# Two transformer layers, float32 weights split in two: weight matmuls that name their columns from the last to the first

## What is computed

```python
proj = rms_norm(x) @ w_in                                   # 2048 x 5448
o    = concatenate([mla(...), fox(...)]) @ w_out            # 2048 x 2048
x    = x + rms_norm(o)
x    = x + 0.5 * (silu(h @ w_gate) * (h @ w_up)) @ w_down   # 2048 x 5632, twice; 5632 x 2048
proj = rms_norm(x) @ w_in_2                                 # mixer, 2048 x 11776
x    = x + merged(attention, spatial gate) @ w_out_2
x    = x + 0.5 * (silu(h @ w_gate) * (h @ w_up)) @ w_down   # second feed-forward block
```

## Time and profile before

| | |
|---|---|
| time, median of 3 runs | 2693.84 us (2693.53 to 2694.23) |
| the profiled execution: its time | 2694.18 us |
| its span, first to last instruction | 2692.4 us |
| mean granted TensorE clock | 0.996 |
| PE busy | 2658.2 us, 99% of the span |
| PEld busy | 2209.8 us, 82% |
| DVE busy | 1430.7 us, 53% |
| ACT busy | 1189.7 us, 44% |
| DMA queue of the weights, share of 16 engines | 56.7% |

### The profile page before, as it was taken

The page is one execution under the profiler, slowest core; times in us unless marked ns, Lnnn a source line. Parts: engine busy times, 40 slices in busy tenths (PEclk is TensorE's granted clock), DMA queues, the critical chain, the costliest instruction groups (busy, mean ns, idle before and its releaser), DMA issues.

```text
span 2692.4 us, 32506 instructions
## 1 busy us (share of the span) xinstructions
PE 2658.2 (99%) x12165; PEld 2209.8 (82%) x12165; DVE 1430.7 (53%) x1562; ACT 1189.7 (44%) x1362; POOL 27.0 (1%) x25
## 2 busy tenths in 40 slices
PE   8999999899999999999999999999999999999998
PEld 6888888788888888888888888888888888888886
DVE  6755555654545455455445655555654454544554
ACT  4544554444444443444444554444444444444333
POOL 0000000000000000000000300000000000000000
PEclk9999999999999999999999999999999999999999
DMA  6655545456565655557665445555566665565554
GB/s 196 204 161 171 158 149 194 149 185 191 188 191 188 188 188 193 190 192 232 190 195 187 147 149 180 192 191 190 185 204 190 189 189 187 187 187 194 195 188 149
DMA packets 258672, 496.23 MB, mean 184 GB/s; under 512 B 17602, under 2 KB 19992, under 8 KB 258328
## 3 DMA queue, kind: packets, MB, share of 16 engines
q1 hardware_dynamic: 257040, 489.81, 56.7%
q0 software_dynamic: 896, 4.89, 0.5%
q10 hardware_dynamic: 648, 0.32, 0.0%
HBM read 492.86 MB, written 2.10 MB: 184 GB/s over the span
## 4 chain that ended last, share of the span: by engine, by line
PE 98%; DVE 1%; DMA 0%; ACT 0%; issue 0%; ACTq 0%; DVEq 0%
PE acc L435 94%; PE tr L451 3%; PE s_ps L490 1%; PE o_ps L513 1%; DVE act_lo L1158 0%; DMA fix<-fixed 0%; PE tr L722 0%; DVE xres L1516 0%; ACT act_hi L813 0%; DVE stats L1178 0%; DVE wlo L1126 0%; DVE u L1692 0%; ACT lat L860 0%; DVE xres L1755 0%; DVE xres L1274 0%
## 5 line engine op out<-in xcount | busy, mean ns | idle before, releaser
L1126 DVE TENSOR_TENSOR wlo<-raw,whi 128x1024 fp32r<-128x1024 f32 x929 | 1135.6, 1225 | 1053.6 <-ACT whi L783 1031.1
L783 ACT ACTIVATE whi<-raw 128x1024 fp32r<-128x1024 f32 x929 | 978.9, 1057 | 1107.8 <-PE acc L435 1101.7
L435 PE MATMUL acc<-whi,act_hi 128*128 128x512 f32 (+1 forms) x2560 | 1008.3, 394 | 6.4 <-DVE wlo L1126 4.3
L435 PE MATMUL acc<-whi,act_lo 128*128 128x512 f32 (+1 forms) x2560 | 996.9, 389 | 0.0
L435 PE MATMUL acc<-wlo,act_hi 128*128 128x512 f32 (+1 forms) x2560 | 995.7, 389 | 0.0
L435 PEld LDWEIGHTS acc<-whi,act_hi 128*128 128x128 f32 x2560 | 481.9, 188 | 102.6 <-issue 5.3
L435 PEld LDWEIGHTS acc<-whi,act_lo 128*128 128x128 f32 x2560 | 481.5, 188 | 100.9
L435 PEld LDWEIGHTS acc<-wlo,act_hi 128*128 128x128 f32 x2560 | 482.2, 188 | 95.3
L435 PE MATMUL acc<-whi,h_hi 128*128 128x512 f32 x704 | 274.3, 390 | 0.0
L435 PE MATMUL acc<-whi,h_lo 128*128 128x512 f32 x704 | 274.0, 389 | 0.0
L435 PE MATMUL acc<-wlo,h_hi 128*128 128x512 f32 x704 | 273.9, 389 | 0.0
(11 more groups left out here) (217 smaller groups left out, 1302.3 us busy)
## 6 DMA issues: line engine op xcount, KB each, us to landing
raw<-in_w_in SPq DMA_DIRECT2D x280, 512.0 KB, 3.5
raw<-in_ffn_w_gate SPq DMA_DIRECT2D x176, 512.0 KB, 4.4
raw<-in_ffn_w_up SPq DMA_DIRECT2D x176, 512.0 KB, 4.2
raw<-in_ffn_w_down SPq DMA_DIRECT2D x176, 512.0 KB, 3.7
raw<-in_w_out SPq DMA_DIRECT2D x64, 512.0 KB, 4.1
raw<-in_w_sg_out SPq DMA_DIRECT2D x24, 512.0 KB, 4.6
raw<-in_w_uq SPq DMA_DIRECT2D x9, 512.0 KB, 4.1
raw<-in_w_ukv SPq DMA_DIRECT2D x8, 512.0 KB, 5.0
```

The source lines that it names most:

```text
L435: last = nc.tensor.matmul(pair[:, half, 0:width], left[:, k, tok], right[:, slot, t, 0:width], start=(k == 0 and n == 0), stop=(j == count ...
L783: nc.scalar.activation(whi[:, slot, :, 0:width], raw[:, slot, :, 0:width], ACT.Copy).then_inc(hi_ready, 1)
L1126: nc.vector.tensor_tensor(wlo[:, slot, :, 0:width], raw[:, slot, :, 0:width], whi[:, slot, :, 0:width].bitcast(F32), ALU.subtract).then_in ...
```

## The change

The matmul at line 435 has two operands whose columns are indexed, the output in `acc` and the moving one in `whi` or `wlo`. Both now run with a step of minus one, from column `width - 1` to column 0. Column c of the moving operand still goes to column c of the output. The stationary operand, the flags, the waits and the order of the instructions stay, and so does every other matmul of the kernel.

```diff
                             for n, (left, right) in enumerate(((hi, whi), (hi, wlo), (lo, whi))):
                                 last = nc.tensor.matmul(
-                                    pair[:, half, 0:width], left[:, k, tok], right[:, slot, t, 0:width],
+                                    pair[:, half, width - 1::-1], left[:, k, tok], right[:, slot, t, width - 1::-1],
                                     start=(k == 0 and n == 0), stop=(j == count - 1 and t == TILES - 1 and n == 2),
                                     skip_group_check=True)
```

## The result

The kernel is slower: 2762.28 us median of 4 runs (2762.06 to 2762.82), against 2693.69 us (2693.50 to 2694.23) for the kernel before on the same chip. The ratio is 1.0256, with a 95% interval of 1.0243 to 1.0269: 68.6 us more. The profiled execution has a span of 2760.6 us at a granted clock of 0.997.

A forecast was written before the change was run, and what follows sets the result against it. PE bounds the kernel: the number of weight matmuls times the distance between starts. Column cost 0, remainder 0 and waits 0 added to the profiled 2694.18 us gave 2694 us; own range 2689 to 2699, stated range 2688 to 5070 us.

The forecast's parts named there:

- the half rate: At each of the 11148 weight matmuls, descending columns go one at a time: 4916 up to 5067 us; chance 0.24.
- the costlier start: At each weight matmul, the first address at the far end costs one more 13.1 ns: 2840 us; chance 0.08.
- What bounds the kernel: PE's weight matmuls at line 435: their number times the distance between starts, 94% of the span; any change comes out undiluted.
- First piece, the column cost: Within each weight matmul, 0.417 ns a column, claimed unchanged by the step's sign: 0, at most 2222 to 2373 us more.
- the lower end, 0: The value taken for the column cost's change in each weight matmul, of a range from 0 to 2222 or 2373 us.
- The price's upper bound: Column cost at one column in the time of two: a wide matmul 200 ns more, in all 2222 to 2373 us.
- The PSUM rule of the Trainium skill: For the matmul output: non-contiguous access slows matmuls significantly, two consecutive elements should be contiguous; read strictly, descending output breaks it.
- Second piece, the remainder of 13.1 ns: Each weight matmul's cost beyond its columns, wide or narrow; change taken as 0, could be 146 us less or more.
- It is paid between two instructions: Reason for leaving the 13.1 ns at 0 change: neither the number nor the kinds of instructions change.
- Its own weight load does not set it: On the 13.1 ns: loads start with the matmul before theirs and last 0.19 us of the 0.227 us.
- Third piece, nobody waits for part of a matmul: Around the weight matmuls: no one waits for single columns, and DVE and ACT splits stay covered by PE; 0.
- wrong in another way: Profile sign outside forecast and rivals: distance right at one width only, or PE waits on `wlo` growing while the distance stays.

## Why the prediction was right or wrong

The stated range, 2688 to 5070 us, holds 2762.28 us, but the forecast itself, 2694 us and no change, is wrong by 68.6 us, well outside its own range of 2689 to 2699. "Slower" had a chance of 0.34. That the stated range holds the result is luck: it reaches so far because of the half rate at its other end, and none of the rivals describes what happened. The nearest in time, the costlier start, was put at 2840 us.

- *What bounds the kernel*: right. The change of the distance came out undiluted, with the same waits and the same work on DVE and ACT.
- *First piece, the column cost; this is the step that failed.* It was put at 0 and was 6.6 ns a wide matmul. "The step's sign changes neither how many values are used of a memory line nor how often a line is left" may be true and doesn't settle it. The order inside a block of 16 bytes is free, as that sentence would have it. The order of the blocks isn't, 226.8 against 233.4 ns. And I took "the lower end, 0" for both sides at once where they had to be held apart: the output side is 0 (ratio 0.9999), the moving side 6.6 ns.
- *The price's upper bound*, 200 to 213 ns a matmul, was 30 times too high. A half rate didn't come, neither for the descending output (2693.33 us) nor for the moving side (2762.53 us).
- *The PSUM rule of the Trainium skill*, which that rival stood on: a descending output is no breach of it that costs time, and neither is one in blocks of four in either mixed order, since those distances (226.8 and 233.4 ns) are the ones that the moving side explains. Two neighbours stayed side by side in all of these; an output that parts them wasn't tried.
- *Second piece, the remainder of 13.1 ns.* The arithmetic from two widths was sound and its reading was not. (The narrow distance of 150.0 ns is also an upper value: within groups of 12 the mean is 149.1 to 149.3.) With 0.417 ns a column and 13.1 ns a start, 256 columns would take 119.8 ns, which is met (119.3), but 448 would take 199.9 and took 204.1, and 504 would take 223.3 and took 226.9. The width of 328 sits on one line (0.455 ns a column) and 512 on another (0.443); drawing a straight line through the two made a start cost out of it. "A costlier start", the rival nearest in time, falls with it: its sign was that wide and narrow are both later by the same ns.
- *"It is paid between two instructions"* and *"Its own weight load does not set it"*: not by its length, indeed, since 32 stationary columns didn't shorten anything. But where it reads does take part: 226.8 against 233.3 ns.
- *Third piece, nobody waits for part of a matmul*: right.
- The list of signs had the true one as "wrong in another way": a distance that is right at one width only, here the narrow one, to within 1 ns.

What stands in its place. Shown: with float32r and reversed, 512 moving columns take 233.3 to 233.6 ns, 0.456 ns each, whatever the shift and the number of stationary columns; ascending with a shift or with fewer stationary columns they take 230 to 233.4 ns. 512 bfloat16 columns beside each other, half the memory, take 216 ns, with the caution above. The kernel before does better than 230, 226.7 ns, where four things come together, and taking any one away loses part or all of it: 16-byte blocks in ascending order, moving tiles on a multiple of 2048 bytes, stationary tiles so too, and 128 stationary columns. The change took away the first. Argued only: that the two reads of PE, of the moving columns and of the weights for the next matmul, meet in the same memory and fall into step where all four hold. The settling behind each job (224 to 236 ns, then 226.7) looks like that, and so do two distances, 230.0 and 233.3 ns, with the same shifted tiles. What in the memory makes them meet, and why a descending order of blocks never falls into step at 512 columns, stays open.

## What to carry to other kernels

Reverse output columns freely, and columns within 16 bytes of a float32 moving operand too, but keep its 16-byte blocks ascending, and with 512 columns place the tiles of both operands of a float32r matmul on a multiple of 2048 bytes: here a shift of the moving tiles by 48 bytes cost 1.9%, most of what the reversal did (2.6%). At other widths measure it: 480 columns took 213.5 ns from a start 48 bytes behind the multiple, and 217.2 ns from the multiple itself. In a kernel that is bound by PE, hold the distance between two starts against what the columns alone would take, at three or more widths: two points always give a straight line. A change that leaves the number and the length of all instructions alone can still cost a few per cent.

## What the runs showed of the hardware that was not expected

- A float32r matmul of 512 columns isn't bound by 2.4 GHz in this kernel (213.3 ns for 512 columns at one each clock): 226.7 or 233.3 ns, against 216.1 ns for 512 bfloat16 columns in half the memory. At half that clock the distance was 427 ns, one column each clock, for either order: so in the kernel before from 488 to 498 us (granted clock 0.51) and in the kernel after from 496 to 506 us (0.51). There the order costs nothing.
- Where the weight load reads from changes how long the matmul beside it takes: 226.8 ns with stationary tiles on a multiple of 2048 bytes and 233.3 ns with others 48 bytes behind one, in the same run and with the same moving tiles. "TensorE: Matmul & The Clock Gate" of the Trainium skill, in its step on LDWEIGHTS, says that loading the next weights doesn't steal read bandwidth from the running matmul; these two numbers speak against taking that as full independence.
- Fewer stationary columns can make the stream slower: 227.0 ns with 128 of them, 231.5 with 32, though the load itself takes 0.11 us instead of 0.19.
- The same matmuls on the same tiles can run at two rates in one execution: 230.0 and 233.3 ns, over 264 of them each, with the moving tiles 48 bytes behind a multiple.
